# Hi and lo parts of the meta tokens as one stationary tile of 32 columns

## The chip, the cores and the metric

The kernel runs on one core of a Trainium2 chip. The metric is the device time of one execution in microseconds (us), lower is better. A core has a matrix engine (TensorE, PE in the rows, with its weight loads shown apart as PEld), VectorE (DVE), ScalarE (ACT), GpSimd (POOL) and SyncE (SP), which here only issues transfers. Each engine works through its own list of instructions in order, and the lists wait for one another on semaphores. All the code shown here is written with the waits and increments by hand; no planner moves an instruction.

## What is computed

An encoder layer runs over two requests (2048 and 512 tokens of 1024 channels), each with the same 16 learned meta tokens put in front of it. The stage that matters here is the first one: normalise, then one combined input projection.

```python
h = jnp.concatenate([meta, x], axis=1)        # 16 meta rows, then the request's tokens
u = _rmsnorm(h, norm1_g)
z = u @ w_in                                  # 1024 -> 3*384 + 384 + 256 columns
xa, gb, gc = z[..., :c0], z[..., c0:2 * c0], z[..., 2 * c0:3 * c0]
xp = z[..., 3 * c0:3 * c0 + POOL_WIDTH]
xf = z[..., 3 * c0 + POOL_WIDTH:]
```

Everything after it (short convolution, pooling, a Fourier mix, the output projection, a SwiGLU and the last norm) is left as it is by the change. The meta rows are the same for both requests, so their part of z is computed once.

## The kernel before, in words

The work runs in stages, one after the other: `project` (the stage of the change, up to about 480 us in the trace), the Fourier part, the output projection, and the two large products of the SwiGLU, which take the rest. To keep near-float32 accuracy each operand is split into a hi part (rounded to the engine's fast 4-byte type, F32R) and a lo part (what is left), and a product is three matmuls, hi*hi, hi*lo and lo*hi, issued by `split_product` (lines 79 to 83).

`project` works on tiles of 128 tokens and blocks of 512 (`T`). Ahead of its loop of five blocks it prepares, in this order on TensorE (lines 619 to 664):

- eight fold groups (line 641), 32 plain float32 matmuls that multiply the pooling weights into the input projection; ACT and DVE split the result into hi and lo (lines 370 and 474);
- four meta groups, the loop over `META_GROUPS`. Each multiplies the 16 meta tokens (stationary operand: `um_hi` or `um_lo`, 128 rows x 16 columns) by four panels of w_in (moving operand: 128 x 512), for the 8 slices of the 1024 channels: 8 x 3 = 24 matmuls into one PSUM bank. The fourth group, which makes the Fourier columns, has two panels (128 x 256) and goes its own way. Group i waits until DVE has made enough lo panels (`w_lo_done` of 4, 8, 9 and 11), and groups 1 to 3 are each followed by the turning of one tile of 128 normalised tokens (`transpose`, line 628: eight 128x128 transposes into banks 6 and 7, from which ACT makes `u_hi` and DVE `u_lo`). A tile's transposes wait until `u_lo` of the tile before has been made, since the two banks are shared. The last tile's transposes follow the fourth group;
- the z turn (line 663). ACT has copied the first three groups' sums (16 rows x 512 columns each, line 377) to `z_meta`, 12 panels side by side on 16 partitions. Twelve transposes bring each panel to 128 partitions x 16 columns in bank 0. ACT copies them into the buffers of the loop (lines 408 and 411), DVE multiplies two of them (lines 502 and 503), and the loop's first matmul waits for that.

Around it ACT works, in a fixed order, through: hi parts of the panels (`w_split`, line 365), the copies out of the meta groups (`z_meta_read_out`, 377), the squares of the token tiles (`square`, 350), from which POOL makes the factor 1/rms (lines 326 and 329), and the hi parts of the turned tiles (`u_tile`, 357). So w_split of panel 8 stands behind the read-out of group 0, and the squares of tiles 2 and 3 stand behind the read-out of group 1, the hi part of tile 0 and panels 9 and 10. DVE has the matching order: the norms (line 453), the lo parts of panels (468) and of tiles (459). `tile(1, t)` is the t-th tile of the first block.

Of the kernel before, what the change touches and what calls it, by code (L numbers as in the profile page):

```python
# [24 lines left out]
ACT = mybir.ActivationFunctionType  # L25
F32 = mybir.dt.float32
F32R = mybir.dt.float32r

P = 128
D = 1024  # L30
KD = D // P
META = 16
# [46 lines left out]
def split_product(pe, out, w, x, first, last):  # L79

    pe.matmul(out, w[0], x[0], start=first, stop=False, skip_group_check=True)  # L81
    pe.matmul(out, w[0], x[1], start=False, stop=False, skip_group_check=True)  # L82
    return pe.matmul(out, w[1], x[0], start=False, stop=last, skip_group_check=True)  # L83
# [71 lines left out]
def project(nc, c, gu, ident, half, eps, tail, tail_stored):  # L155
# [9 lines left out]
    with ExitStack() as ctx:  # L165
        sb = lambda n, s, d=F32: ctx.enter_context(nc.sbuf_tensor(n + "_sb", s, d))
        sem = lambda n: ctx.enter_context(nc.semaphore(n))
        w_hi = sb("w_in_hi", [P, NPAN + 5, KD, P], F32R)
        w_lo = sb("w_in_lo", [P, NPAN + 5, KD, P], F32R)
        u_hi = sb("u_hi", [P, KD, T], F32R)  # L170
        u_lo = sb("u_lo", [P, KD, T], F32R)
        um_hi = sb("u_meta_hi", [P, KD, META], F32R)
        um_lo = sb("u_meta_lo", [P, KD, META], F32R)
        xt = sb("x_tiles", [P, NT, D])
        junk = sb("junk", [P, D])
        g1 = sb("norm1_rows", [P, D])
# [8 lines left out]
        win = sb("window_sums", [P, 4, W])  # L185
# [5 lines left out]
        bank = ctx.enter_context(nc.psum_tensor("proj_bank", [P, 8, 512], F32))  # L191

        flat = lambda a: a.rearrange("p t n -> p (t n)")
# [2 lines left out]
        wp = [a[0:GROUP] for a in (flat(win[:, :, :])[:, 0:D], flat(win[:, :, :])[:, D:2 * D], flat(res[:, :, :]),  # L196
                                   xt[:, NT - 1, :])]
        pw = xa[0:GROUP, 0:4 * GROUP].rearrange("p (g o) -> p g o", g=4)
        z_meta = flat(win[0:META, :, :])

        consts = sem("consts_landed")
        raw_landed = [sem(f"raw_landed{i}") for i in range(RAW)]
# [38 lines left out]
        def tile(r, t):  # L241
            return 4 * r - 3 + t
# [99 lines left out]
        def _(act):  # L342
# [30 lines left out]
            def z_meta_read_out(i):  # L373

                j, n = META_GROUPS[i]
                act.wait_ge(z_meta_done, i + 1)
                act.activation(z_meta[:, P * j:P * (j + n)], bank[0:META, 4 + i % 2, 0:P * n], ACT.Copy)\
                    .then_inc(z_meta_read, 1)


# [6 lines left out]
            for n in range(4, 8):  # L387
                w_split(n)
            z_meta_read_out(0)
            square(1, 0)  # L390
            square(1, 1)
            w_split(8)
            z_meta_read_out(1)
            u_tile(1, 0)
            for n in (9, 10):
                w_split(n)
            square(1, 2)
            square(1, 3)
            z_meta_read_out(2)
            u_tile(1, 1)  # L400
            act.wait_ge(xf_done, 1)
# [5 lines left out]
            part = lambda i: bank[:, 0, 3 * META * i:3 * META * (i + 1)]  # L407
# [210 lines left out]
        def _(pe):  # L618
            pe.wait_ge(consts, 16 * 7)

            def transpose(n, t, rows=P):

                pe.wait_ge(normed, n + 1)
                for h in range(2):
                    if not isinstance(n, int) or n:
                        pe.wait_ge(u_lo_made, 2 * n + h - 1)
                    for k in range(4):
                        ins = pe.transpose(bank[:, 6 + h, P * k:P * k + rows],
                                           xt[0:rows, t, (4 * h + k) * P:(4 * h + k + 1) * P],
                                           ident[0:rows, 0:rows])  # L630
                    ins.then_inc(transposed, 1)
# [4 lines left out]
            for n in range(8):  # L636
# [3 lines left out]
                for k in range(4):  # L640
                    ins = pe.matmul(bank[:, n % 4, k * GROUP:(k + 1) * GROUP],
                                    wp[g][:, (4 * h + k) * P:(4 * h + k + 1) * P], pw[:, g, :],
                                    start=True, stop=True)
# [3 lines left out]
            for i, (j, n) in enumerate(META_GROUPS):  # L647
                pe.wait_ge(w_lo_done, (4, 8, 9, 11)[i])
                if i == 2:
                    pe.wait_ge(fold_lo, 8)  # L650
                if i >= 2:
                    pe.wait_ge(z_meta_read, i - 1)
                for k in range(KD):
                    ins = split_product(pe, bank[0:META, 4 + i % 2, 0:P * n].rearrange("p (a n) -> p a n", a=n),
                                        (um_hi[:, k, :], um_lo[:, k, :]),
                                        [w[:, j:j + n, k, :] for w in (w_hi, w_lo)], k == 0, k == KD - 1)
                ins.then_inc(z_meta_done if i < 3 else xf_done, 1)
                if i:
                    transpose(tile(1, i - 1), i - 1)
            transpose(tile(1, NT - 1), NT - 1)  # L660
            pe.wait_ge(z_meta_read, 3)
            for j in range(NPAN + 3):
                ins = pe.transpose(bank[:, 0, META * j:META * (j + 1)], z_meta[:, P * j:P * (j + 1)],
                                   ident[0:META, 0:META])
            ins.then_inc(panel_done, 12)

            def body(r, more):
# [1441 lines left out]
```

## Time and profile before

| | us |
|---|---|
| median of 3 runs | 2550.61 |
| lowest and highest of them | 2545.59 and 2553.97 |
| the profiled execution, its time | 2544.79 |
| the profiled execution, its span from first to last instruction | 2543.2 |
| TensorE busy | 2408.1 |
| stage with the meta groups, until the loop's first matmul | 60.80 |

The profile is one execution, so its times are differences within 2543.2 us, with 1.6 us around it. A row of the timeline is one run of like instructions; its start counts from the span's first instruction. The duration of a matmul in a row is from its issue to its modelled end; matmuls overlap, so the pace is read from the distance between starts. A float32 matmul that is no transpose leaves two records (the 32 fold matmuls are 64 records). PEclk in the rows is the share of the TensorE clock that was granted: 1.00 is 2.4 GHz and 0.50 is 1.2 GHz. The record of it begins at 34.1 us; ahead of that the column says 1.00 whatever the clock was, and the distance between the matmuls tells it.

### The profile page before, as it was taken

How to read it: one execution, taken by the hardware profiler on the slowest of the kernel's cores; microseconds unless marked ns; L12 is line 12 of the kernel's file. 1: busy time of each engine (PE TensorE's matmuls, PEld its weight loads, DVE VectorE, ACT ScalarE, POOL GpSimd, SP SyncE). 2: the span in 40 equal slices, each digit the busy share in tenths (PEclk: the TensorE clock that was granted, in tenths of full speed). 3: DMA queues.
4: the chain of work that ended last, by engine and by line, in shares of the span. 5: the costliest groups of instructions: out<-in, count | busy, mean ns of one | idle time of the engine just before them, and what ended most of it. 6: DMA issues, size and time to landing. Idle time of an engine off the chain costs nothing. (4 is left out here: it accounts for less than half of the span.)

```text
span 2543.2 us, 32577 instructions
## 1 busy us (share of the span) xinstructions
PE 2408.1 (95%) x11786; PEld 2151.0 (85%) x11786; DVE 1548.3 (61%) x2312; ACT 903.1 (36%) x1486; POOL 361.0 (14%) x509
## 2 busy tenths in 40 slices
PE   6999999788999679999999999999999999999997
PEld 4887888677887579999899999899999888888886
DVE  4443545555877465655765555855555575686775
ACT  4121211242443343333433333433333333444543
POOL 0110110006444001111011111111111000100101
PEclk9999999888999889999999999999999999999999
DMA  5556862265565456666677765454545886687874
GB/s 185 210 133 165 215 200 60 92 204 196 212 240 211 172 166 193 218 211 202 187 222 221 219 201 165 142 167 156 158 155 165 295 255 192 208 303 224 270 228 138
DMA packets 216058, 492.95 MB, mean 194 GB/s; under 512 B 27552, under 2 KB 60866, under 8 KB 207469
## 3 DMA queue, kind: packets, MB, share of 16 engines
q1 hardware_dynamic: 188301, 358.99, 43.0%
q0 software_dynamic: 27616, 132.11, 17.4%
q8 instruction: 85, 1.39, 0.2%
q14 instruction: 56, 0.46, 0.1%
HBM read 395.90 MB, written 164.31 MB: 220 GB/s over the span
## 5 line engine op out<-in xcount | busy, mean ns | idle before, releaser
L81 PE MATMUL gu_bank<-v_form_hi_sb,gu_hi_sb 128*128 128x428 f32 (+1 forms) x1848 | 663.2, 359 | 40.2 <-DVE gu_lo_sb L1806 17.3
L82 PE MATMUL gu_bank<-v_form_lo_sb,gu_hi_sb 128*128 128x428 f32 (+1 forms) x1848 | 661.1, 358 | 0.0
L83 PE MATMUL gu_bank<-v_form_hi_sb,gu_lo_sb 128*128 128x428 f32 (+1 forms) x1848 | 660.6, 357 | 0.0
L1714 ACT ACTIVATE gu_hi_sb<-gu_raw_sb 128x512 fp32r<-128x512 f32 x462 | 286.1, 628 | 362.9 <-PE gu_bank L83 362.9
L1806 DVE TENSOR_TENSOR gu_lo_sb<-gu_raw_sb,gu_hi_sb 128x512 fp32r<-128x512 f32 x462 | 311.1, 686 | 162.1 <-ACT gu_hi_sb L1714 162.1
L81 PEld LDWEIGHTS gu_bank<-v_form_hi_sb,gu_hi_sb 128*128 128x128 f32 x1848 | 349.5, 189 | 59.2 <-issue 24.7
L83 PEld LDWEIGHTS gu_bank<-v_form_hi_sb,gu_lo_sb 128*128 128x128 f32 x1848 | 349.7, 189 | 11.5
L82 PEld LDWEIGHTS gu_bank<-v_form_lo_sb,gu_hi_sb 128*128 128x128 f32 x1848 | 349.8, 189 | 11.0
L81 PE MATMUL gu_bank<-gu_hi_sb,act_hi_sb 128*128 128x512 f32 x770 | 303.9, 395 | 3.5 <-DVE act_lo_sb L1898 3.5
L83 PE MATMUL gu_bank<-gu_hi_sb,act_lo_sb 128*128 128x512 f32 x770 | 302.4, 393 | 0.0
L82 PE MATMUL gu_bank<-gu_lo_sb,act_hi_sb 128*128 128x512 f32 x770 | 299.7, 389 | 0.0
L1893 DVE TENSOR_TENSOR gu_lo_sb<-gu_raw_sb,gu_hi_sb 128x1024 fp32r<-128x1024 f32 x116 | 141.4, 1219 | 157.2 <-ACT gu_hi_sb L1750 157.2
L1750 ACT ACTIVATE gu_hi_sb<-gu_raw_sb 128x1024 fp32r<-128x1024 f32 x116 | 122.5, 1056 | 295.4 <-PE gu_bank L83 258.3
L81 PE MATMUL proj_bank<-u_hi_sb,w_in_hi_sb 128*128 128x512 f32 x480 | 189.3, 394 | 7.6 <-DVE u_lo_sb L459 6.5
L82 PE MATMUL proj_bank<-u_lo_sb,w_in_hi_sb 128*128 128x512 f32 x480 | 188.4, 392 | 0.0
L83 PE MATMUL proj_bank<-u_hi_sb,w_in_lo_sb 128*128 128x512 f32 x480 | 188.4, 392 | 0.0
L1677 POOL DMA_DIRECT2D act_forms<-act_left_sb x66 | 36.4, 551 | 1001.0 <-DVE act_sums_sb L1854 1001.0
L83 PEld LDWEIGHTS gu_bank<-gu_hi_sb,act_lo_sb 128*128 128x128 f32 x770 | 145.0, 188 | 33.9
L81 PEld LDWEIGHTS gu_bank<-gu_hi_sb,act_hi_sb 128*128 128x128 f32 x770 | 145.2, 189 | 33.0 <-DVE gu_lo_sb L1893 3.9
L82 PEld LDWEIGHTS gu_bank<-gu_lo_sb,act_hi_sb 128*128 128x128 f32 x770 | 144.8, 188 | 32.3
L81 PE MATMUL out_bank<-w_panel_hi_sb,v_hi_sb 128*128 128x512 f32 x320 | 128.8, 402 | 7.2 <-DVE h_sb L1347 7.2
L1898 DVE TENSOR_TENSOR act_lo_sb<-act_raw_sb,act_hi_sb 128x384 fp32r<-128x384 f32 (+1 forms) x231 | 132.1, 596 | 0.7 <-ACT act_hi_sb L1757 0.7
(190 smaller groups left out, 3288.4 us busy)
## 6 DMA issues: line engine op xcount, KB each, us to landing
gu_raw_sb<-gu_sums SPq DMA_DIRECT2D x264, 256.0 KB, 4.1
gu_raw_sb<-w_gu_q SPq DMA_DIRECT2D x198, 256.0 KB, 2.7
gu_sums<-w_gu_q POOLq DMA_DIRECT2D x24, 1408.0 KB, 14.3
gu_raw_sb<-down_sums SPq DMA_DIRECT2D x132, 256.0 KB, 3.7
act_raw_sb<-act_forms SPq DMA_DIRECT2D x154, 192.0 KB, 3.7
gu_raw_sb<-w_down_q SPq DMA_DIRECT2D x99, 256.0 KB, 3.3
w_raw_sb<-w_panels SPq DMA_DIRECT2D x40, 512.0 KB, 3.6
act_raw_sb<-act_forms SPq DMA_DIRECT2D x77, 256.0 KB, 4.2
```

The lines of the kernel that those rows point to most:

```text
L81: pe.matmul(out, w[0], x[0], start=first, stop=False, skip_group_check=True)
L82: pe.matmul(out, w[0], x[1], start=False, stop=False, skip_group_check=True)
L83: return pe.matmul(out, w[1], x[0], start=False, stop=last, skip_group_check=True)
L1677: pool.dma_start(c["act_forms"][f, m, :, at:at + n], src[:, 0:n]).then_inc(a_stored, 16)
L1714: act.activation(w_hi[:, s, :], raw[:, s, :], ACT.Copy).then_inc(w_hi_made, 1)
L1750: act.activation(w_hi[:, s:e, :], raw[:, s:e, :], ACT.Copy).then_inc(w_hi_made, 1)
L1806: dve.tensor_tensor(w_lo[:, s, :], raw[:, s, :], w_hi[:, s, :].bitcast(F32), ALU.subtract)\
L1893: dve.tensor_tensor(w_lo[:, s:e, :], raw[:, s:e, :], w_hi[:, s:e, :].bitcast(F32), ALU.subtract)\
L1898: dve.tensor_tensor(a_lo[:, s, 0:w], a_raw[:, s, 0:w], a_hi[:, s, 0:w].bitcast(F32), ALU.subtract)\
```

## The change

The two meta tiles become one of 32 columns, hi in columns 0 to 15 and lo in 16 to 31. In meta groups 0 to 2 one matmul with the 32 columns against w_hi makes hi*hi in PSUM rows 0 to 15 and lo*hi in rows 16 to 31, and a second one with the 16 hi columns adds hi*lo to rows 0 to 15: two matmuls for three. `z_meta` holds both halves on 32 partitions, and ACT's read-out takes 32 rows. Where z is turned, each transpose is replaced by two plain float32 matmuls that add up in PSUM, one with the columns of the identity that pick the upper half, one with those that pick the lower. The fourth group is as before.

```diff
-        um_hi = sb("u_meta_hi", [P, KD, META], F32R)
-        um_lo = sb("u_meta_lo", [P, KD, META], F32R)
+        um = sb("u_meta", [P, KD, 2 * META], F32R)
+        um_hi, um_lo = um[:, :, 0:META], um[:, :, META:2 * META]
...
-        z_meta = flat(win[0:META, :, :])
+        z_meta = flat(win[0:2 * META, :, :])
...
-                act.activation(z_meta[:, P * j:P * (j + n)], bank[0:META, 4 + i % 2, 0:P * n], ACT.Copy)\
+                act.activation(z_meta[:, P * j:P * (j + n)], bank[0:2 * META, 4 + i % 2, 0:P * n], ACT.Copy)\
                     .then_inc(z_meta_read, 1)
...
+                out = lambda rows: bank[0:rows, 4 + i % 2, 0:P * n].rearrange("p (a n) -> p a n", a=n)
                 for k in range(KD):
-                    ins = split_product(pe, bank[0:META, 4 + i % 2, 0:P * n].rearrange("p (a n) -> p a n", a=n),
-                                        (um_hi[:, k, :], um_lo[:, k, :]),
-                                        [w[:, j:j + n, k, :] for w in (w_hi, w_lo)], k == 0, k == KD - 1)
+                    wk = [w[:, j:j + n, k, :] for w in (w_hi, w_lo)]
+                    if i < 3:
+
+                        pe.matmul(out(2 * META), um[:, k, :], wk[0], start=k == 0, stop=False, skip_group_check=True)
+                        ins = pe.matmul(out(META), um_hi[:, k, :], wk[1], start=False, stop=k == KD - 1,
+                                        skip_group_check=True)
+                    else:
+                        ins = split_product(pe, out(META), (um_hi[:, k, :], um_lo[:, k, :]), wk, k == 0, k == KD - 1)
...
             for j in range(NPAN + 3):
-                ins = pe.transpose(bank[:, 0, META * j:META * (j + 1)], z_meta[:, P * j:P * (j + 1)],
-                                   ident[0:META, 0:META])
+                for part in range(2):
+                    ins = pe.matmul(bank[:, 0, META * j:META * (j + 1)], z_meta[:, P * j:P * (j + 1)],
+                                    ident[0:2 * META, META * part:META * (part + 1)], start=part == 0, stop=part == 1)
             ins.then_inc(panel_done, 12)
```

## Rows read from the trace of the kernel before

**Rows 1.** The page: busy time of each engine over the whole span, share of span, instructions.

```profile
PE 2408.1 (95%) x11786; PEld 2151.0 (85%) x11786; DVE 1548.3 (61%) x2312; ACT 903.1 (36%) x1486; POOL 361.0 (14%) x509
```

**Rows 2.** The list of waits, 28 to 64 us: who for whom, total us, times, longest.

```profile
PE proj_bank L81 <- DVE w_in_lo_sb L468: 1.8, 1, 1.8
```

**Rows 3.** The timeline of PE, 31 to 62 us: start, duration, line, tiles, shape, count, idle.

```profile
31.60 0.63 PE L82 MATMUL proj_bank<-w_in_lo_sb,u_meta_hi_sb 128*16 128x512 f32 x1
...
33.31 0.63 PE L83 MATMUL proj_bank<-w_in_hi_sb,u_meta_lo_sb 128*16 128x512 f32 x1
...
40.04 0.40 PE L81 MATMUL proj_bank<-w_in_hi_sb,u_meta_hi_sb 128*16 128x512 f32 x1 [1.81 <-DVE w_in_lo_sb L468]
...
45.60 1.04 PE L628 MATMUL proj_bank<-ident_sb,x_tiles_sb 128*128 128x128 f32 x8
46.39 0.48 PE L81 MATMUL proj_bank<-w_in_hi_sb,u_meta_hi_sb 128*16 128x512 f32 x1
...
52.01 1.04 PE L628 MATMUL proj_bank<-ident_sb,x_tiles_sb 128*128 128x128 f32 x8
52.80 0.36 PE L81 MATMUL proj_bank<-w_in_hi_sb,u_meta_hi_sb 128*16 128x256 f32 x1
...
55.62 1.03 PE L628 MATMUL proj_bank<-ident_sb,x_tiles_sb 128*128 128x128 f32 x8
57.73 1.16 PE L628 MATMUL proj_bank<-ident_sb,x_tiles_sb 128*128 128x128 f32 x8 [1.07 <-DVE u_lo_sb L459]
58.82 0.91 PE L663 MATMUL proj_bank<-ident_sb,window_sums_sb 16*128 16x16 f32 x12
60.80 0.50 PE L81 MATMUL proj_bank<-u_hi_sb,w_in_hi_sb 128*128 128x512 f32 x1 [1.07 <-DVE gated_sb L503]
```

**Rows 4.** The timeline of DVE, 38 to 58 us, same columns.

```profile
38.76 1.23 DVE L468 TENSOR_TENSOR w_in_lo_sb<-outer_gate_sb,w_in_hi_sb 128x1024 fp32r<-128x1024 f32 x1 [2.26 <-ACT w_in_hi_sb L365]
...
44.38 1.22 DVE L468 TENSOR_TENSOR w_in_lo_sb<-z_pool_sb,w_in_hi_sb 128x1024 fp32r<-128x1024 f32 x1
...
54.59 1.28 DVE L459 TENSOR_TENSOR u_lo_sb<-proj_bank,u_hi_sb 128x512 fp32r<-128x512 f32 x2
56.89 1.29 DVE L459 TENSOR_TENSOR u_lo_sb<-proj_bank,u_hi_sb 128x512 fp32r<-128x512 f32 x2 [1.02 <-ACT u_hi_sb L357]
```

**Rows 5.** The timeline of ACT, 45 to 51 us, and a copy in the loop.

```profile
45.80 0.59 ACT L377 ACTIVATE window_sums_sb<-proj_bank 16x512 f32<-16x512 f32 x1 [3.35 <-PE proj_bank L83]
...
50.37 1.06 ACT L350 ACTIVATE junk_sb<-x_tiles_sb 128x1024 f32<-128x1024 f32 x1
...
128.02 0.60 ACT L430 ACTIVATE z_pool_sb<-proj_bank 128x512 f32<-128x512 f32 x1 [4.76 <-PE proj_bank L83]
```

**Rows 6.** The z turn's line: count, ns min/median/max, first and last start, forms.

```profile
L663 PE MATMUL proj_bank<-ident_sb,window_sums_sb x12: 207/208/229, 58.8 to 59.5; 16*128 16x16 f32 x12
```

**Rows 7.** The timeline of PE at three runs of plain float32 matmuls.

```profile
14.52 7.14 PE L641 MATMUL proj_bank<-xa_sb,window_sums_sb 96*128 96x96 f32 x32 [4.58 <-DMA x_tiles_sb<-w_pool_T]
...
597.45 2.69 PE L1411 MATMUL out_bank<-group_means_sb,mix_squares_sb 128*128 128x1 f32 x12 [3.34 <-PEq L795]
...
649.80 1.48 PE L1411 MATMUL out_bank<-group_means_sb,mix_squares_sb 128*128 128x1 f32 x12
```

**Rows 8.** Stretches by window: length, busy time by engine, granted clock (PEclk), DMA share, GB/s.

```profile
61.50:64.70 3.20, 3.20 (x9) 2.48 (x8) 0.00 (x0) 0.00 (x0) 0.00 (x0) 0.50 0.81 309
64.90:68.00 3.10, 3.10 (x16) 2.53 (x15) 0.00 (x0) 0.00 (x0) 0.00 (x0) 1.00 0.16 61
...
652.00:655.00 3.00, 3.00 (x9) 2.32 (x8) 3.00 (x4) 1.80 (x3) 0.00 (x0) 0.50 0.30 70
860.20:863.50 3.30, 1.26 (x9) 0.80 (x8) 2.69 (x4) 1.15 (x2) 1.29 (x3) 1.00 0.63 256
863.60:867.00 3.40, 3.40 (x18) 3.23 (x17) 2.96 (x3) 2.40 (x5) 1.94 (x2) 0.51 0.06 23
867.00:870.00 3.00, 1.33 (x12) 1.09 (x10) 0.00 (x0) 2.07 (x4) 0.00 (x0) 1.00 0.00 1
```

## The prediction

> **What bounds the kernel now.** I read the page first: TensorE is busy 2408.1 of 2543.2 us [rows 1], so time on TensorE's path counts, but the share says nothing of the first 61 us, where the change lies. The views for that are the list of waits and the timelines of TensorE, DVE and ACT for 28 to 62 us.
>
> The list of waits for 28 to 64 us names as TensorE's longest one 1.8 us for the lo part of a weight panel [rows 2]. The timeline of TensorE [rows 3] says where: it stands still for 1.81 us after group 0, until group 1 starts at 40.04, released by DVE, whose split of panel 7 runs from 38.76 for 1.23 us, to 39.99 [rows 4]; ahead of it DVE itself had waited 2.26 us. From 40.04 to 55.62 TensorE has no gap: group 1 until 45.60, eight transposes, group 2 from 46.39 to 52.01, eight transposes, group 3 from 52.80, the third tile's transposes at 55.62. Then comes a round trip (transposes, ACT's hi part, DVE's lo part at 56.89 [rows 4]), which releases the last transposes at 57.73 after 1.07 us of waiting; the turn of z from 58.82 for 0.91 us; ACT and DVE; the loop's first matmul at 60.80. From there everything hangs on TensorE, so what moves 60.80 moves the end.
>
> A second chain runs beside TensorE. ACT's read-out of group 1 at 45.80 had waited for it [rows 5]; behind it in ACT's order stand the hi part of tile 0, panels 9 and 10, and the squares of tiles 2 and 3, the last at 50.37 [rows 5]. From these POOL and DVE make the norms, and then DVE the lo part of tile 1 from 54.59 [rows 4], for which the transposes at 55.62 need to wait.
>
> The pace of a matmul depends on the clock. Between 31.60 and 33.31 four starts take 1.71 us, 0.43 each; in group 1, 24 take 5.56 us, 0.232 each [rows 3]. The loop shows both again: from 61.5 to 64.7 the granted clock is 0.50 (1.2 GHz) with TensorE fully busy, after 64.9 it is 1.00 (2.4 GHz) [rows 8]. It fell after the thin stretch from 57 to 61 us, in which TensorE did transposes, the turn, and waited [rows 3].
>
> **Part by part.** *Group 0* loses 8 of 24 matmuls. At 0.232 us that is 1.9 us, at 0.43 us 3.4. None of it arrives: group 1 waits for panel 7 until 39.99 either way, on a chain of loads and splits that does not ask for group 0. TensorE's idle time ahead of group 1 grows from 1.81 to 3.7 us or more.
>
> *Group 1* loses 8 x 0.232 = 1.9 us and has nothing ahead of its end but TensorE. But the longer idle time has a price. Between 860.2 and 863.5 TensorE was busy for 1.26 of 3.3 us, and from 863.6 the clock stood at 0.51 [rows 8]; in the 3.7 us before 40.04 it would do nothing at all. If the clock falls there, as at 61.5, a low stretch like that one holds some eight matmuls, each 0.2 us longer: 1.6 us. I take a gain of 0.3 us, and 1.9 as the other end.
>
> *Group 2* loses 1.9 us too, and no time is gained by that: its successor on the path, the lo part of tile 1, comes out of ACT's and POOL's chain, which moves only with group 1's end. The first half of that lo part is ready at about 54.59 + 0.65 - 0.3 = 54.95, the second at 55.6, against transposes that now start at 55.62 and take half a us a half. With both halves counted the turn of z starts 0.5 us earlier, at about 58.3 (2.1 us earlier, at 56.7, if the clock stays up in group 1). Panel 8's lo part at 44.38 + 1.22 = 45.6 [rows 4] is what group 2 could wait for; it doesn't move.
>
> *Read-out.* ACT reads 32 rows instead of 16; its time goes with the 512 columns, not its rows: 0.59 us for 16 rows, 0.60 for 128 in the loop [rows 5]. Nothing. A stationary tile of 32 columns for 16 costs nothing either: its load is hidden under the matmul before, at 16 columns in group 1 as at 128 in the loop, where the pace is the same.
>
> *The turn of z* is the large term. Now 12 transposes start over 0.7 us, 62 ns apart, with 0.21 us for the last [rows 3, 6]. After the change there are 24 plain float32 matmuls, 48 records. No row shows this shape. The nearest are the group means [rows 7]: plain float32, stationary 128 columns, a moving operand of one column. Twelve records take 1.48 us at the upper level, so 11 steps of 112 ns and 0.25; at the lower level 2.69 us, steps of 213 ns. That this is nearly twice a transpose although less is moved says the weight load sets the pace, and that load is the same here (128 columns). So 47 x 0.112 + 0.25 = 5.5 us at the upper level, 47 x 0.213 + 0.35 = 10.4 at the lower; at the pace of the transposes, the other bound, 47 x 0.062 + 0.2 = 3.1. The Trainium skill (FP8 and Floating Point Precision, TensorE Precision Notes) says that true float32 makes four passes through the array; as four steps of a transpose each, an estimate, the turn would take 24 x 4 x 62 ns = 6.0 us. The trace shows two records per matmul, and the sum goes by their 112 ns.
>
> Which level? Group 3 ends at 53.4; after it TensorE has only 16 transposes and the turn. Before, the same stretch from 55.62 on, with the wait that follows the turn, brought the clock down by 61.5, and it was down from 652.0 on, right behind a run of group means [rows 8]. The turn is now 5 us or more longer, so the fall comes inside it, at its start in some executions, near its end in others. I take the middle, 8.0 us, which is 7.1 more than 0.91.
>
> *Behind the turn* the loop's first matmuls ran at the lower level before, for 3.3 us, which cost 1.6 [rows 8]. After the change they meet the clock already down, and it rises only after dense work: one such stretch to two, 1.6 to 3.3 us. I add 0.5; the ends are -1.6 (it never falls) and +1.7.
>
> Sum: -0.5 + 7.1 + 0.5 = +7.1 us. No later wait hides it: the loop's loads, norms and stores are all released by TensorE's progress. The profiled execution would go from 2544.79 to 2551.9. It lies 5.8 us below the median, which goes from 2550.61 to **2557.7**.
>
> **The rivals.** *Clock low through the whole turn* (the other side: slower by more than can be missed). If the two runs of eight transposes don't hold the clock, it is down before the turn starts, which then takes 10.4 us, 9.5 more; with group 1's gain at 0.5 and two low stretches in the loop (+1.7) that is +10.7, **2561.3**. It decides from the point where the clock falls before 58.3 us. For it: only 2 us of transposes in the 5 us before. Against: between 863.6 and 867 TensorE did transposes alone, at 0.51, and then the clock stood at 1.00 [rows 8], so transposes can lift it. The Trainium skill (TensorE: Matmul & The Clock Gate, Part 4) says that transposes don't count as busy for the clock; by that rule this rival is what happens, and the row at 867 speaks against the rule. I give it 0.22.
>
> *Clock high through the turn.* Then it takes 5.5 us (+4.6), and the gain ahead is 0.5 or 2.1: +2.5 to +4.1, **2553.9**. For it: the turn is real matrix work, 5 us without a gap. Against: the fall behind the group means. 0.12.
>
> *Cheap turn.* If the weight load of 32 rows runs at the transposes' pace (16 rows there, 128 in the group means), the turn takes 3.1 us, +2.2, and group 1's gain, 0.5 to 2.1, makes up for most: +0.1 to +1.7, **2551.5**. Against it: the fold matmuls, plain float32 on 96 rows, take 7.14 us for 32 records at the lower level, (7.14 - 0.42)/31 = 217 ns a step against 213 on 128 rows [rows 7], so fewer rows buy nothing there. 0.08.
>
> *The saving arrives whole.* 24 matmuls x 0.232 = 5.6 us, less at least 2.2 for the turn, is -3.4; even that is 0.13% of 2550. So a measurable gain has no mechanism here; I leave 0.02 for it.
>
> **How the numbers follow.** The forecast has 0.58. About 0.3% (7.65 us) is what a measurement of this kernel can tell from no change, and +7.1 lies just under it: with runs 8 us apart and +5 to +9 for the place of the fall, I put 0.42 of the forecast's chance above it, 0.9 of the low rival's, none of the others': 0.45 slower, 0.02 faster, 0.53 the same. The range is from 2549 (cheap turn, lower runs) to 2564 (low throughout, upper runs).
>
> **What would show it.** The turn's line with 48 records, 112 or 213 ns apart, over 7 to 9 us; group 1 still starting at 40.0, with part of its matmuls 0.43 apart; the lo part of tile 1 within 0.5 us of its old time; the loop's first matmul 6 to 7 us after 60.80; the lower clock level around the turn. It is wrong if the turn takes less than 4 us, if the loop starts earlier than before, or if a later wait takes the delay up.

## The result, and the profile after

The changed kernel takes 2552.45 us (median of 20 runs, 2546.84 to 2557.65) against 2546.58 for the kernel before in the same runs (20 of them, 2540.89 to 2554.47). The ratio is 1.0022, with a 95% interval of 1.0012 to 1.0033: slower by 5.6 us, 3 to 8 by the interval. The forecast was +7.1 us (+0.28%).

The profiled execution of the changed kernel took 2552.47 us, its span is 2550.9, so 7.7 more than the span before. The timeline of TensorE for its first stage (start, duration, line, tiles, shape, count, idle before), which answers to [rows 3]:

```profile
36.81 0.39 PE L659 MATMUL proj_bank<-w_in_lo_sb,u_meta_sb 128*16 128x512 f32 x1
41.80 0.45 PE L658 MATMUL proj_bank<-w_in_hi_sb,u_meta_sb 128*32 128x512 f32 x1 [4.60 <-DVE w_in_lo_sb L468]
...
42.47 0.63 PE L658 MATMUL proj_bank<-w_in_hi_sb,u_meta_sb 128*32 128x512 f32 x1
42.90 0.63 PE L659 MATMUL proj_bank<-w_in_lo_sb,u_meta_sb 128*16 128x512 f32 x1
...
47.08 1.03 PE L628 MATMUL proj_bank<-ident_sb,x_tiles_sb 128*128 128x128 f32 x8
...
51.65 1.03 PE L628 MATMUL proj_bank<-ident_sb,x_tiles_sb 128*128 128x128 f32 x8
...
56.89 1.16 PE L628 MATMUL proj_bank<-ident_sb,x_tiles_sb 128*128 128x128 f32 x8 [1.48 <-DVE u_lo_sb L459]
59.02 1.87 PE L628 MATMUL proj_bank<-ident_sb,x_tiles_sb 128*128 128x128 f32 x8 [0.97 <-DVE u_lo_sb L459]
60.82 10.42 PE L670 MATMUL proj_bank<-ident_sb,window_sums_sb 32*128 32x16 f32 x48
72.30 0.80 PE L81 MATMUL proj_bank<-u_hi_sb,w_in_hi_sb 128*128 128x512 f32 x1 [1.07 <-DVE gated_sb L503]
```

Read it against [rows 3] by distances between starts. Group 1 starts 1.76 us later than before, only because panel 7 landed later in this execution, so times are best taken from its start. Group 0 now ends with the matmul at 36.81, and TensorE is idle for 4.60 us where it was 1.81. Group 1 takes 5.28 us from 41.80 to 47.08, against 5.56 before, although it has 16 matmuls for 24: its starts are 0.43 us apart in the first half. The transposes and group 2 take 4.57 us from 47.08 to 51.65, for 6.41. The last two tiles' transposes each wait for DVE (1.48 us, and 0.97 at the second), and the second eight take 1.87 us for 1.16. So the turn starts 19.0 us after group 1, against 18.8 before: in this execution nothing of the 24 matmuls is left. The turn itself has 48 records and 10.42 us, for 12 and 0.91, and the loop starts 30.5 us after group 1, against 20.8.

The list of waits, 28 to 75 us, answers to [rows 2] (total us, times, longest):

```profile
PE proj_bank L658 <- DVE w_in_lo_sb L468: 4.6, 1, 4.6
...
PE proj_bank L628 <- DVE u_lo_sb L459: 2.4, 2, 1.5
```

Both of TensorE's waits have grown, from 1.8 and 1.1 us: it has less to do and waits for the same others. The stretches by window (length, busy time by engine, PEclk, DMA share, GB/s) answer to [rows 8]:

```profile
42.20:45.40 3.20, 3.20 (x9) 1.10 (x8) 1.75 (x2) 2.00 (x3) 2.12 (x4) 0.50 0.51 164
59.20:60.80 1.60, 1.60 (x8) 1.28 (x7) 0.37 (x2) 0.60 (x1) 0.00 (x0) 0.50 0.99 407
60.80:71.20 10.40, 10.40 (x49) 10.31 (x48) 1.28 (x2) 0.60 (x1) 0.00 (x0) 0.50 0.31 118
72.30:76.00 3.70, 3.70 (x9) 2.93 (x10) 0.00 (x0) 0.00 (x0) 0.00 (x0) 0.50 0.00 0
76.50:79.00 2.50, 2.50 (x12) 2.05 (x11) 0.00 (x0) 0.00 (x0) 0.00 (x0) 1.00 0.00 0
```

The granted clock is at 0.50 (1.2 GHz) in the first half of group 1, and again from 59.2 us, during the last transposes, through the whole turn and for the first 4 us of the loop. The line of the turn, as in [rows 6]:

```profile
L670 PE MATMUL proj_bank<-ident_sb,window_sums_sb x48: 369/369/391, 60.8 to 70.9; 32*128 32x16 f32 x48
```

From there the delay is carried. The first Fourier columns of the loop's first block come at 139.5 us (127.8 before), the Fourier stage's first matmul at 496.0 (484.6), so 11.7 and 11.4 us later, 1.76 of it panel 7. In the Fourier stage 3 us come back, and the output projection ends 7.9 later (all by starts of its matmuls). The change touches neither; the same Fourier stage takes 109.1 and 111.9 us in two traces of the kernel before, and between 106.1 and 111.9 over all thirteen traces of this study, so those 3 us are within what executions differ by there.

### The profile page after: what moved, and what is told of

The parts are those of the page before. It is cut to its first block and busy times, and to the rows that moved or that the text cites. A ratio compares the mean times of both kernels' runs of the same rounds, so it can differ in the third digit from the quotient of the medians.

```text
span 2550.9 us, 32601 instructions
## 1 busy us (share of the span) xinstructions
PE 2414.8 (95%) x11798; PEld 2158.7 (85%) x11798; DVE 1548.7 (61%) x2312; ACT 903.0 (35%) x1486; POOL 359.3 (14%) x509
## 5 line engine op out<-in xcount | busy, mean ns | idle before, releaser
L83 PEld LDWEIGHTS gu_bank<-v_form_hi_sb,gu_lo_sb 128*128 128x128 f32 x1848 | 349.7, 189 | 11.4
```

## The experiments

The question is not only whether the turn costs what it should, but where the groups' saving went, and whether the clock's place in it is a cause or a bystander. Theory: the turn pays for itself alone, by records, 112 ns each at the upper level of the clock and 213 at the lower; the groups' saving is real but makes TensorE's work thinner, and the clock's fall takes it back. Rivals: the loss lies in the groups or the read-out; the turn's pace has nothing to do with the clock; ACT's and DVE's chain sets the loop's start anyway.

This table puts all traces beside each other, in us, by starts in the timeline of TensorE: from the start of group 1 to the turn, the turn's length, from group 1 to the loop's first matmul, from there to the first Fourier columns (the first block's panels, 65.4 with the clock up throughout), and from group 1 to there in all. The last column is the measured ratio to the kernel before, with its 95% interval. Where it is empty there was one run each: 2550.14 us (e9), 2546.16 (e10) and 2550.74 (e11), beside 2546.19 for the kernel before. The kernel before alone differs by 4 us between two such runs, so these three single times say nothing here, and only the traces of e9 to e11 are used.

| kernel | to the turn | turn | to the loop | first block | in all | ratio |
|---|---|---|---|---|---|---|
| before | 18.78 | 0.91 | 20.76 | 67.0 | 87.8 | 1 |
| before, again (e9) | 21.54 | 0.91 | 23.52 | 68.3 | 91.8 | |
| change | 19.02 | 10.42 | 30.50 | 67.2 | 97.7 | 1.0022 (1.0012 to 1.0033) |
| change, again (e7) | 16.73 | 8.36 | 26.16 | 66.8 | 93.0 | 1.0020 (1.0007 to 1.0033) |
| change, third (e11) | 19.52 | 7.17 | 27.76 | 68.0 | 95.8 | |
| turn alone (e1) | 18.80 | 7.59 | 27.46 | 67.6 | 95.1 | 1.0033 (1.0020 to 1.0046) |
| half of the turn (e10) | 18.96 | 2.85 | 22.88 | 66.9 | 89.8 | |
| groups alone (e2) | 18.83 | 1.46 | 21.35 | 67.9 | 89.2 | 1.0009 (0.9999 to 1.0020) |
| sum by DVE (e3) | 18.80 | 1.48 | 21.64 | 66.8 | 88.4 | 1.0017 (1.0008 to 1.0026) |
| change, 8 fillers (e4) | 18.88 | 10.42 | 30.37 | 67.4 | 97.7 | 1.0037 (1.0023 to 1.0051) |
| sum by DVE, fillers (e5) | 16.75 | 0.93 | 19.47 | 65.4 | 84.9 | 0.9992 (0.9980 to 1.0003) |
| change, fillers (e6) | 16.76 | 6.58 | 24.96 | 66.7 | 91.6 | 1.0017 (1.0004 to 1.0029) |
| before, fillers (e8) | 18.96 | 0.91 | 20.94 | 65.4 | 86.4 | 0.9990 (0.9980 to 0.9999) |

### e1: the turn alone

```diff
 for j in range(NPAN + 3):
-    ins = pe.transpose(bank[:, 0, META * j:META * (j + 1)], z_meta[:, P * j:P * (j + 1)],
-                       ident[0:META, 0:META])
+    for part in range(2):
+        ins = pe.matmul(bank[:, 0, META * j:META * (j + 1)], z_meta[:, P * j:P * (j + 1)],
+                        ident[0:META, META * part:META * (part + 1)], start=part == 0, stop=part == 1)
```

> The kernel before, with three matmuls per slice in the meta groups as ever, and only the turn of z made as in the change: 24 plain float32 matmuls on 16 rows, the second of each pair with a zero part of the identity, so the sums are right. Theory (the turn is the whole cost, the groups give almost nothing): the turn's line has 48 records and takes 5.5 to 10.4 us against 0.91; the loop's first matmul 6 to 10 us after that of the kernel before on the same chip, once a later or earlier landing of panel 7 is taken off; time +5 to +9 us (ratio 1.002 to 1.0035). Rival (the turn is cheap at 62 ns a record, the loss lies in the groups or in the read-out of 32 rows): turn 3.1 us, time within 2 us of before.

Ratio 1.0033, +8.4 us. The turn in the timeline, and the stretches around it:

```profile
58.83 7.59 PE L664 MATMUL proj_bank<-ident_sb,window_sums_sb 16*128 16x16 f32 x48
67.48 0.80 PE L81 MATMUL proj_bank<-u_hi_sb,w_in_hi_sb 128*128 128x512 f32 x1 [1.07 <-DVE gated_sb L503]
```

Stretches of the same kernel by window:

```profile
58.90:61.90 3.00, 3.00 (x28) 3.00 (x28) 1.29 (x2) 0.63 (x2) 0.00 (x0) 1.00 0.89 341
62.10:66.00 3.90, 3.90 (x20) 3.90 (x20) 0.00 (x0) 0.00 (x0) 0.00 (x0) 0.50 0.67 257
```

Everything ahead of the turn is as before, to 0.02 us. The clock fell at 62.0, inside the turn: 28 of its steps are short, 19 long, 28 x 0.112 + 19 x 0.213 = 7.2 us, and with the last record's tail the 7.59 of the row. The loop starts 6.7 us later and, at the lower level until 72, loses 0.6 more. The turn is the large cost; the rival (a cheap turn of 3.1 us) falls.

### e2: the groups alone

The change, with the turn by transposes of the upper 16 rows, so that the lo*hi part of the meta tokens is left out of the result:

```diff
-                for part in range(2):
-                    ins = pe.matmul(bank[:, 0, META * j:META * (j + 1)], z_meta[:, P * j:P * (j + 1)],
-                                    ident[0:2 * META, META * part:META * (part + 1)], start=part == 0, stop=part == 1)
+                ins = pe.transpose(bank[:, 0, META * j:META * (j + 1)], z_meta[0:META, P * j:P * (j + 1)],
+                                   ident[0:META, 0:META])
```

> The change's groups alone: 32 columns against w_hi, 16 against w_lo, read-out of 32 rows; but z is turned by 12 transposes of the upper 16 rows as before, so the lo*hi part of the meta tokens is left out of the result. Theory: group 0's saving is idle time; group 1 starts where panel 7's lo part releases it and has 0.43 us between some of its starts, since the clock fell in the longer idle time; the turn of z starts 0.3 to 0.7 us earlier relative to panel 7 than in the kernel before; time -0.5 us, not to be told from before (ratio 0.999 to 1.001). Rival (the saving arrives, the turn eats it): the turn starts 3.7 to 5.6 us earlier, time -4 us (ratio 0.9985).

Ratio 1.0009: no gain, and the interval reaches further to a loss. 24 matmuls fewer, and the loop starts 0.6 us later after group 1 than before. The timeline of TensorE:

```profile
39.52 0.64 PE L658 MATMUL proj_bank<-w_in_hi_sb,u_meta_sb 128*32 128x512 f32 x1 [2.82 <-DVE w_in_lo_sb L468]
...
54.35 1.16 PE L628 MATMUL proj_bank<-ident_sb,x_tiles_sb 128*128 128x128 f32 x8 [1.49 <-DVE u_lo_sb L459]
56.48 1.94 PE L628 MATMUL proj_bank<-ident_sb,x_tiles_sb 128*128 128x128 f32 x8 [0.97 <-DVE u_lo_sb L459]
58.35 1.46 PE L669 MATMUL proj_bank<-ident_sb,window_sums_sb 16*128 16x16 f32 x12
60.87 0.79 PE L81 MATMUL proj_bank<-u_hi_sb,w_in_hi_sb 128*128 128x512 f32 x1 [1.06 <-DVE gated_sb L503]
```

Stretches of the same kernel by window:

```profile
39.60:42.00 2.40, 2.40 (x6) 0.87 (x7) 1.28 (x1) 2.22 (x5) 1.70 (x3) 0.50 0.68 215
56.00:58.00 2.00, 1.52 (x8) 1.55 (x8) 0.93 (x2) 0.54 (x2) 0.00 (x0) 0.50 0.97 375
61.00:66.00 5.00, 5.00 (x12) 3.94 (x13) 0.00 (x0) 0.00 (x0) 0.00 (x0) 0.50 0.17 66
```

Group 1 starts at the lower level. By the transposes at 54.35 the kernel is 0.75 us ahead of before, counted from group 1. Then the clock falls at 56, with TensorE busy only in pieces; the last transposes take 1.94 us for 1.16, the turn 1.46 for 0.91, and the first 5 us of the loop stay at 0.50. The turn was expected to start 0.3 to 0.7 us earlier and starts 0.05 us later: I had not charged the fall to the transposes themselves.

### e3: the halves summed by DVE

```diff
-                for part in range(2):
-                    ins = pe.matmul(bank[:, 0, META * j:META * (j + 1)], z_meta[:, P * j:P * (j + 1)],
-                                    ident[0:2 * META, META * part:META * (part + 1)], start=part == 0, stop=part == 1)
+                ins = pe.transpose(bank[:, 0, 2 * META * j:2 * META * (j + 1)], z_meta[:, P * j:P * (j + 1)],
+                                   ident[0:2 * META, 0:2 * META])
...
+            halves = bank[:, 0, 0:24 * META].rearrange("p (j h n) -> p j n h", j=12, h=2)
+            dve.wait_ge(panel_done, 12)
+            dve.reduce_sum(res[:, 1, 0:12 * META].rearrange("p (j n) -> p j n", j=12), halves,
+                           axis=mybir.AxisListType.X).then_inc(z_summed, 1)
```

ACT's four copies and DVE's two products then read the sums from `res`.

> The change, but the halves are summed by DVE: 12 transposes of 32 rows leave 12 x 32 columns in PSUM, one reduction adds the halves into a buffer, and ACT's copies and DVE's products read that. Theory: the turn takes 0.8 to 1.0 us again, the reduction 0.4 to 0.6 us in place of ACT's first copy, the loop starts within 1 us of where e2_groups starts it; time as before or up to 2 us less (ratio 0.999 to 1.0005), that is 4 to 8 us less than the change. Rival (any sum of halves on the path costs what the change costs): ratio 1.002.

In the trace the order of things is as the theory has it: 12 records, the loop 0.3 us behind e2's. The turn takes 1.48 us where 0.8 to 1.0 was expected, as in e2, since the clock had fallen ahead of it, at 57.6.

The turn and the loop's first matmul in the timeline:

```profile
58.67 1.48 PE L675 MATMUL proj_bank<-ident_sb,window_sums_sb 32*128 32x32 f32 x12
61.52 0.79 PE L81 MATMUL proj_bank<-u_hi_sb,w_in_hi_sb 128*128 128x512 f32 x1 [1.36 <-ACT z_pool_sb L412]
```

But the ratio is 1.0017, where 0.999 to 1.0005 was expected: a miss. The trace's own excess over the profiled execution before (span 2545.8 against 2543.2) does not lie here: the Fourier stage's first matmul comes 0.1 us earlier, the stage ends at the same 593.7, and 2.4 us are lost in the output projection, 273.0 us against 270.6, which the edit does not touch. Why it took longer there in this kernel I cannot say; it stays open. So the measured times alone do not show that a turn without plain matmuls is faster than the change: the intervals of the two ratios overlap. That the turn is the cost rests on e1 and on the rows.

### e4: eight fillers behind group 0

The change with eight matmuls of 128x512 behind group 0, into the bank that group 1 starts afresh; the same work in group 0 as before, a third of it thrown away.

```diff
+                if i == 0:
+                    for d in range(8):
+                        pe.matmul(bank[0:META, 5, :].rearrange("p (a n) -> p a n", a=4), um_hi[:, 0, :],
+                                  w_hi[:, 0:4, 0, :], start=True, stop=True, skip_group_check=True)
```

> The change, and behind group 0 eight matmuls of 128x512 into the bank that group 1 starts afresh, so that TensorE is idle ahead of group 1 no longer than in the kernel before; their result is thrown away. Theory: the clock stays at its upper level there, group 1 takes 3.7 us (0.232 between starts) in place of some 5, and the turn of z starts 1.2 to 1.8 us earlier relative to panel 7 than in the change; the turn still has 48 records over 5.5 to 10.4 us; time 1 to 2 us less than the change. Rival (group 1 is slow for another reason: its loads or its moving operand): group 1 keeps starts of 0.43 us.

Group 1's starts were 0.43 us apart again, which the expectation gave to the rival, and the ratio is 1.0037 where 1 to 2 us less than the change was expected: a miss on both counts. Its timeline:

```profile
40.08 0.42 PE L658 MATMUL proj_bank<-w_in_hi_sb,u_meta_sb 128*32 128x512 f32 x1 [2.06 <-DVE w_in_lo_sb L468]
...
45.37 1.04 PE L628 MATMUL proj_bank<-ident_sb,x_tiles_sb 128*128 128x128 f32 x8
```

Stretches of the same kernel by window:

```profile
38.20:40.00 1.80, 0.00 (x0) 0.00 (x0) 1.20 (x1) 1.80 (x3) 0.00 (x0) 1.00 0.95 335
40.60:43.80 3.20, 3.20 (x9) 1.25 (x8) 1.86 (x2) 1.88 (x3) 2.06 (x3) 0.50 0.48 164
```

But the window view shows why: 2.06 us of idle time, hardly more than the 1.81 of before, went with a fall of the clock to 0.50 at 40.5. So an equal gap is no guarantee: the same gap costs nothing in one execution and 1.6 us in another. It is not the loads or the moving operand, since e7 ran the same group 1 at 0.23 us a start. The experiment did not do what it was meant for; e5 and e6 fill more.

### e5 and e6: fillers wherever TensorE waits in this stage

`filler(b, n)` issues n such matmuls into bank b. e5 puts it into e3, e6 into the change (there with 4 at the last place).

```diff
+                if i == 0:
+                    filler(5, 12)
+                if i == 3:
+                    filler(3, 2)
                 if i:
                     transpose(tile(1, i - 1), i - 1)
+            filler(3, 4)
             transpose(tile(1, NT - 1), NT - 1)
...
             ins.then_inc(panel_done, 12)
+            filler(3, 6)
```

> e3_sum_reduce with TensorE kept at dense work where it waits in this stage: matmuls of 128x512 whose result is thrown away, 12 behind group 0, 2 behind group 3, 4 between the last two token tiles' transposes and 6 behind the turn. Theory (the groups' saving is real but the thinner work lets the clock fall, in group 1 and from some 57 us on, and gives it back): no start of group 1 is 0.43 us behind the last, the granted clock is 1.00 from group 1 to the loop's first panels, the turn takes 0.9 to 1.0 us, the loop starts 19 to 19.5 us after group 1's start (before 20.76, e3_sum_reduce 21.64) and runs at the upper level at once; time 3 to 4 us below the kernel before (ratio 0.9985 to 0.999) and 6 to 8 below e3_sum_reduce. Rival (DVE's and ACT's chain sets the loop's start, the clock has no part in it): loop start within 0.3 us of e3_sum_reduce's 21.6 us, ratio 1.001 to 1.002.

> The change itself with the same throw-away matmuls (12 behind group 0, 2 behind group 3, 4 between the last two tiles' transposes, 4 behind the turn). Theory: the turn's 48 records start at the upper level, 112 ns apart, and the clock can fall only inside it; the turn takes 5.5 to 8 us in place of the 10.4 of the profiled change; the loop starts 23.5 to 27 us after group 1 (the change 30.5); time 3 to 5 us below the change, still above before (ratio 1.0005 to 1.002). Rival (the turn's pace is not the clock's): 213 ns between the starts all the same.

e5, timeline and windows:

```profile
41.81 0.41 PE L669 MATMUL proj_bank<-w_in_hi_sb,u_meta_sb 128*32 128x512 f32 x1 [2.34 <-DVE w_in_lo_sb L469]
...
45.53 1.03 PE L634 MATMUL proj_bank<-ident_sb,x_tiles_sb 128*128 128x128 f32 x8
47.43 0.41 PE L669 MATMUL proj_bank<-w_in_hi_sb,u_meta_sb 128*32 128x512 f32 x1 [0.86 <-DVE w_in_lo_sb L469]
...
58.56 0.93 PE L685 MATMUL proj_bank<-ident_sb,window_sums_sb 32*128 32x32 f32 x12
...
61.28 0.50 PE L81 MATMUL proj_bank<-u_hi_sb,w_in_hi_sb 128*128 128x512 f32 x1 [0.30 <-ACT z_pool_sb L412]
```

Stretches of the same kernel by window:

```profile
42.00:45.00 3.00, 3.00 (x14) 1.33 (x13) 1.33 (x2) 2.12 (x4) 2.25 (x4) 1.00 0.52 175
61.30:64.70 3.40, 3.40 (x15) 2.80 (x16) 0.00 (x0) 0.00 (x0) 0.00 (x0) 1.00 0.78 296
```

The clock stands at 1.00 throughout, group 1 takes 3.72 us, the turn starts 16.75 us after it, 2.0 earlier than before, and the loop at 19.47, as expected, and at the upper level at once. Group 2 at 47.43 now waits for panel 8's lo part. In all the first stage is 2.9 us shorter than in the first trace before, 3.5 than e3's. The rival (ACT's and DVE's chain decides) falls. The measured ratio is 0.9992, a smaller gain than the 0.9985 to 0.999 expected, and not clear of 1.

The 12 matmuls behind group 0 are not shown to have done their part: TensorE still stood idle for 2.34 us ahead of group 1, longer than the 2.06 us of e4, and in e7 the clock stayed up in group 1 without any filler. What the fillers do show comes later: the wait between the last two tiles' transposes is gone, and the clock did not fall at all in e5 and e8, and in e6 not before the turn.

e6: the turn starts 16.76 us after group 1 too. Its row in the timeline:

```profile
56.69 6.58 PE L680 MATMUL proj_bank<-ident_sb,window_sums_sb 32*128 32x16 f32 x48
```

38 of its steps are short and 9 long: the clock fell some 4.3 us (38 x 0.112) into it. That is the same code as the change's 10.42 us, at another level of the clock, so the pace is the clock's. In all 91.6 us, against 93.0 to 97.7 in the three traces of the change. The time was expected 3 to 5 us below the change. The ratios, 1.0017 and 1.0020, can't tell the two apart: here the traces carry the verdict, not the times.

### e7 and e11: the change twice more

> The change once more, unaltered, on the chip of these runs, so that the others have it beside them. Theory: ratio 1.002 to 1.0035; the turn of 48 records again takes more than 7 us, and the place where the clock falls (before the turn, or inside it) sets whether it is nearer 7.5 or 10.4. Rival (the profiled change was an odd execution): a turn below 6 us.

> The change a third time, for its trace. Theory: the turn takes 7.5 us if the clock falls inside it and 10.4 if before it; from group 1's start to the first Fourier columns 93 to 98 us, as in the other two traces (97.7 and 93.0), against 87.8 before. Rival (something else than the turn scatters between the two): a time in which turn and total don't go together, for instance a turn of 10.4 with 93.

e7's timeline of TensorE:

```profile
39.61 0.42 PE L658 MATMUL proj_bank<-w_in_hi_sb,u_meta_sb 128*32 128x512 f32 x1 [3.24 <-DVE w_in_lo_sb L468]
...
43.34 1.04 PE L628 MATMUL proj_bank<-ident_sb,x_tiles_sb 128*128 128x128 f32 x8
...
56.34 8.36 PE L670 MATMUL proj_bank<-ident_sb,window_sums_sb 32*128 32x16 f32 x48
```

e11's timeline:

```profile
39.70 0.63 PE L658 MATMUL proj_bank<-w_in_hi_sb,u_meta_sb 128*32 128x512 f32 x1 [2.88 <-DVE w_in_lo_sb L468]
...
46.17 1.04 PE L628 MATMUL proj_bank<-ident_sb,x_tiles_sb 128*128 128x128 f32 x8
...
59.22 7.17 PE L670 MATMUL proj_bank<-ident_sb,window_sums_sb 32*128 32x16 f32 x48
```

The ratio of e7 is 1.0020; its trace is of the fastest of its eleven runs (2548.46 us, their median 2552.62). Turn and total do not go together here: e11 has the shorter turn (7.17) and the longer stage (95.8 against 93.0), as the rival of e11 asked. The rows say where it comes from: group 1 takes 6.47 us in e11 and 3.73 in e7. The clock fell ahead of group 1 in e11, which made the stage up to the turn 2.8 us longer, but then it was up for the first 32 steps of the turn, until 62.8; in e7 it stayed up in group 1 and fell after 20 steps, at 58.6. So it is not another cause but the other place of the same one.

### e8: fillers in the kernel before

The same `filler`, 6 behind group 0, 4 between the last two tiles' transposes, 4 behind the turn, no other change.

> The kernel before with throw-away matmuls alone: 6 behind group 0, 4 between the last two tiles' transposes, 4 behind the turn. Theory: the loop starts 20.8 us after group 1 as before, but at the upper level, which saves the 1.7 us that the low stretch behind 61.4 us cost; time 0 to 2 us below before (ratio 0.9992 to 1.0002). Rival (fillers hold the matmuls behind them up): loop start 0.5 us or more later, ratio above 1.0005.

Ratio 0.9990, interval 0.9980 to 0.9999, where 0.9992 to 1.0002 was expected. Its timeline of TensorE:

```profile
40.76 0.40 PE L81 MATMUL proj_bank<-w_in_hi_sb,u_meta_hi_sb 128*16 128x512 f32 x1 [1.98 <-DVE w_in_lo_sb L468]
...
59.72 0.91 PE L673 MATMUL proj_bank<-ident_sb,window_sums_sb 16*128 16x16 f32 x12
...
61.70 0.50 PE L81 MATMUL proj_bank<-u_hi_sb,w_in_hi_sb 128*128 128x512 f32 x1
```

The stretch of the same kernel that answers to the first one of [rows 8]:

```profile
61.50:64.70 3.20, 3.17 (x14) 2.51 (x14) 0.14 (x2) 0.00 (x0) 0.00 (x0) 1.00 0.83 306
```

The first block takes 65.4 us for 67.0: the 1.6 us of the low stretch behind 61.5 [rows 8] are gone, and the loop starts only 0.2 us later after group 1. It is the one kernel of this study whose interval lies below the kernel before, by very little for one of nine such comparisons; and its first stage is 1.4 us shorter than in the first trace before, where the ratio says 2.5. Against e5, which has the fillers too, its first stage is 1.4 us longer (86.35 and 84.91, one trace each): that is what the groups' saving and the sum by DVE are worth when the clock stays up, too little for the ratios, 0.9992 and 0.9990, to show.

### e9: the kernel before, again

> The kernel before, unaltered, for a second trace of it. From the start of group 1 to the loop's first Fourier columns (the end of the first block's panels) it took 87.8 us in the first trace. Theory (the first stage repeats but for the place of the clock's fall): 86 to 89 us, turn 0.9 to 1.5 us, the clock at its lower level at some time between 57 and 66 us or not at all. Rival (the executions scatter so much that single traces can't be compared): more than 3 us away from 87.8.

The timeline of TensorE:

```profile
40.41 0.61 PE L81 MATMUL proj_bank<-w_in_hi_sb,u_meta_hi_sb 128*16 128x512 f32 x1 [3.37 <-DVE w_in_lo_sb L468]
...
48.56 1.04 PE L628 MATMUL proj_bank<-ident_sb,x_tiles_sb 128*128 128x128 f32 x8
```

Stretches of the same kernel by window:

```profile
36.90:39.00 2.10, 0.13 (x1) 0.00 (x0) 0.00 (x0) 0.96 (x1) 0.00 (x0) 1.00 0.89 314
39.40:46.00 6.60, 5.59 (x14) 1.91 (x15) 4.66 (x4) 3.31 (x6) 2.24 (x4) 0.50 0.27 101
```

In all 91.8 us, where 86 to 89 was expected, and 4.0 from the first trace: the rival's number. Here too it is the clock: in this execution group 0 ended early, TensorE was idle for 3.37 us, the clock fell at 39.3, and group 1 took 8.15 us with its 24 matmuls, for 5.56. Single traces of this stage must not be compared in their totals, then, but row by row with the granted clock beside them.

### e10: half of the turn

The kernel before with its 12 transposes as 12 plain matmuls.

```diff
-    ins = pe.transpose(bank[:, 0, META * j:META * (j + 1)], z_meta[:, P * j:P * (j + 1)],
-                       ident[0:META, 0:META])
+    ins = pe.matmul(bank[:, 0, META * j:META * (j + 1)], z_meta[:, P * j:P * (j + 1)],
+                    ident[0:META, 0:META], start=True, stop=True)
```

> The kernel before with its 12 transposes of the turn made as 12 plain float32 matmuls on 16 rows: 24 records, half of the change's turn, nothing else. Theory (cost by records, 112 ns at the upper and 213 ns at the lower level): turn 23 x 0.112 + 0.25 = 2.8 us at the upper level, up to 5.2 at the lower; since TensorE is dense until 55.6 us the clock is still up for most of it, so 2.8 to 4 us; from group 1's start to the first Fourier columns 2 to 4.5 us more than before. Rival (the adding up of two matmuls in one place of PSUM makes the turn slow, not the plain float32): turn about 1 us.

The turn in the timeline:

```profile
59.08 2.85 PE L663 MATMUL proj_bank<-ident_sb,window_sums_sb 16*128 16x16 f32 x24
```

24 records, 2.85 us, (2.85 - 0.25)/23 = 113 ns a step, all at the upper level. No two matmuls add up in one place here, so adding up is not what costs; it is plain float32 in place of a transpose: 2.85 us for 0.91 with the same shapes, and as much again, and more, for the second half of each pair. In all 89.8 against 87.8, at the lower end of the 2 to 4.5 us more that were expected.

## Why the prediction came out

The forecast was 2557.7 us by +7.1 on the median of the three runs shown, 2550.61. The measured median is 2552.45, in the range. Of the 5.3 us between the two, 4.0 are the median of before, which over 20 runs is 2546.58. The shift, +5.9 us by the medians and +5.6 by the ratio, is 1.2 to 1.5 short of the sum. The loop was to start 6 to 7 us later; by distance from group 1 it starts 9.7, 5.4 and 7.0 us later in the three traces of the change. The lo part of tile 1 was to stay within 0.5 us; in the first trace it starts 0.3 us earlier. About 0.3% was called the least that can be told from no change; 20 runs each told 0.22% from none. The chances given to the five outcomes add up to 1.02. Point by point:

- *Group 0, nothing.* Right. The idle time ahead of group 1 is 4.60, 3.24 and 2.88 us in the three traces of the change, where 3.7 or more was forecast. In the kernel before it is 1.81 and 3.37.
- *Group 1, 0.3 us of 1.9 with the clock falling, 1.9 without.* Right at both ends: 5.28 us in the first trace (0.28 gained), 3.73 in e7 (1.83). In e11 it was 6.47, a loss of 0.9, beyond the end that I gave, and the kernel before can lose as much: 8.15 in e9. The term is a draw between executions on both sides, and I had charged it to the change alone. It is not an even draw, though. Of the four traces with the old groups and no fillers (before, e9, e1, e10) group 1 met the lower level in one, of the five with the new groups and no fillers (the change three times, e2, e3) in four. Up to the turn the old groups take 18.78, 21.54, 18.80 and 18.96 us, 19.5 in the mean, the new ones 19.02, 16.73, 19.52, 18.83 and 18.80, 18.6 in the mean: some 0.9 us of the saving arrive, where 0.5 was forecast, as far as nine traces can tell. This is the mis-sized term: it was counted against a trace in which the clock happened to stay up.
- *Group 2, nothing, since the lo part of tile 1 is next.* Right: 1.48 us of waiting for it in two traces of the change, and with the clock up a wait for panel 8 ahead of that (0.86 us in e5, 0.85 in e7).
- *The turn, 8.0 us between 5.5 and 10.4.* Right: 10.42, 8.36 and 7.17, mean 8.65. The step that carried it, taking the 112 and 213 ns of the group means [rows 7] rather than the 62 of the transposes, held to a nanosecond (113 in e10, 213 in the first trace). The Trainium skill (FP8 and Floating Point Precision, TensorE Precision Notes) says that true float32 makes four passes through the array. At a transpose's pace, an estimate, I had 6.0 us at the upper level from that; e10 measures 113 ns for each of two records, so 226 ns a matmul where four such steps are 248. The rows were the better price.
- *Behind the turn, +0.5.* The first block took 67.2, 66.8 and 68.0 us after the change, 67.0 and 68.3 before: nothing to be seen.
- *The sum.* The first stage takes 95.5 us in the mean of the three traces of the change and 89.8 in that of the two before, 5.7 more; against the first profile alone it is 7.7. That 5.7 is close to the measured 5.6 is partly luck: one of the two traces before has the fall in group 1, more than its one in four above, and the whole times of the same five executions differ by 3.1 us only, as the stages behind scatter too. The sum came near in part because its misses cancel: in the means, the turn took 0.65 us more than the 8.0 that I took, the groups gave 0.4 more back, and the 0.5 behind the turn is not there.
- *The rival with the clock low through the whole turn* was what the profiled execution did (and e4), so a chance of 0.22 was on the low side, but one of the three traces of the change is no rule either. The Trainium skill (TensorE: Matmul & The Clock Gate, Part 4) says that the upper level of the clock does not engage for transposes. The rise at 867 us, behind a stretch of transposes alone [rows 8], speaks against that. The stretch of transposes and short waits ahead of the turn did not hold it in the first trace, where it fell at 59.1, and held it beyond the end of the transposes in e7 and e11; since TensorE also stood still there, these runs don't decide whether the transposes or the waits let it fall.
- *The clock high through the turn.* This did not happen in any of the six traces with 48 records (the change three times, e1, e4, e6): the clock fell ahead of the turn or inside it, and never rose in it, although TensorE was busy from its first record to its last.
- *The cheap turn, and a saving that arrives whole.* Neither happened. The groups' saving can arrive: 2 us of it do at the turn's start in e5, with throw-away work, and in e7, without it, the clock being up in group 1 in both.

## What to carry to other kernels

Replacing a transpose by a plain float32 matmul was dear here, however little it moved: 0.226 us for one at the upper level of the clock, against 0.062. Count the records and price each by a row of plain float32 with a stationary operand of the same width. A saving on an engine that then waits can be worth less than nothing. In e2 the clock fell in the longer waits and slowed the very next group, the transposes and the start of the loop, and that ate all of a saving of 24 matmuls; in the change it left about 1 us of it. Before a term that hangs on the clock is charged to a change, look whether the kernel before does not pay it too, in a second trace and in every other trace that has the stage unaltered.

## What the hardware showed that I had not expected

Behind a gap of 2.06 us on TensorE the clock fell to 0.50 in e4, and within one of 2.88 in e11; it did not with 1.81 in the first trace before, with 2.34 in e5 or with 3.24 in e7. The length of the gap alone doesn't decide it. A busy engine doesn't either: in the turn of the first trace TensorE was busy for 10.40 of 10.40 us and the clock stayed at 0.50, and it rose only 3.9 us into the loop; in e1 the clock fell in the middle of a turn without a gap. And work that is thrown away may pay: with 14 useless matmuls in the kernel before, the clock stood at 1.00 from group 1 into the loop in the trace, and the ratio is 0.9990 (0.9980 to 0.9999), which is hardly clear of 1.
